# Attention weights scaled before they are transposed, a bit search counted by two engines in turn, and a sink as a column of the logits

## What is computed

```
def sink_softmax(logits, sinks):
    m = max(max(logits, axis=-1), s)
    e = exp(logits - m)
    return e / (sum(e, axis=-1) + exp(s - m))
# A: _, sel = top_k(scores, topk);  p = softmax(q @ k_sel / 8 + bias);  o = p @ v_sel
# B: logits = q @ k / 8 + bias (window mask);  p = sink_softmax(logits, sinks);  o = p @ v
```

## Time and profile before

| | |
|---|---|
| median of 3 runs | 2345.16 us (2342.01 to 2346.71) |
| profiled execution | 2343.02 us, span of its profile 2341.2 us |
| prompt's attention of A, first maximum to first sample logits L836 | 596.6 to 731.8 us |
| prompt's attention of B, first logits to L912 | 1763.8 to 1844.5 us |
| TensorE busy over the span | 96% |

### The profile page before, as it was taken

How to read it: one execution, slowest core, us unless ns; L and a number is a source line. 1 busy time by engine, 2 the same in 40 slices (tenths; PEclk the granted TensorE clock), 3 DMA queues, 4 the chain that set the end, 5 groups by cost and what they waited for, 6 DMA issues and landing times.

```text
span 2341.2 us, 39794 instructions
## 1 busy us (share of the span) xinstructions
PE 2258.6 (96%) x14801; PEld 2029.8 (87%) x14819; DVE 1137.1 (49%) x1811; ACT 415.4 (18%) x848; POOL 1029.7 (44%) x622
## 2 busy tenths in 40 slices
PE   7999999999888899999999999999999999999997
PEld 6999989959666588999999999999996689999997
DVE  4544522488584546555512555542264465555311
ACT  3101000131554412010000101000015420101002
POOL 4546455414001024555555555555541055555552
PEclk9999999999799999999999999999999899999998
DMA  5435363535003433333223333322350023333221
GB/s 125 99 73 115 78 155 89 114 64 147 10 1 100 130 89 77 86 81 81 78 84 90 82 86 85 81 78 82 94 154 23 1 73 81 81 86 83 79 83 60
DMA packets 378042, 196.33 MB, mean 84 GB/s; under 512 B 66531, under 2 KB 374476, under 8 KB 377932
## 3 DMA queue, kind: packets, MB, share of 16 engines
q1 hardware_dynamic: 366108, 180.79, 31.3%
q10 hardware_dynamic: 11552, 13.71, 2.0%
q0 software_dynamic: 288, 0.56, 0.1%
HBM read 192.23 MB, written 11.64 MB: 87 GB/s over the span
## 4 chain that ended last, share of the span: by engine, by line
PE 61%; DVE 2%; ACTq 0%; ACT 0%; issue 0%; DVEq 0%
PE psum L594 17%; PE psum L597 11%; PE psum L595 10%; PE psum L593 10%; PE psum L596 9%; PE psum L749 1%; PE psum L775 1%; DVE XS L1448 1%; PE psum L745 1%; PE psum L789 1%; ACTq L1200 0%; PE psum L758 0%; DVE squares L1481 0%; PE psum L939 0%; PE psum L938 0%
## 5 line engine op out<-in xcount | busy, mean ns | idle before, releaser
L545 POOL CAST WSP<-WST 128x1024 fp32r<-128x1024 f32 (+1 forms) x305 | 310.5, 1018 | 1250.0 <-PE psum L597 1008.8
L547 POOL TENSOR_TENSOR WSP<-WST,WSP 128x1024 fp32r<-128x1024 f32 (+1 forms) x305 | 709.3, 2326 | 24.5
L594 PE MATMUL psum<-XS,WSP 128*128 128x512 f32 x1672 | 658.4, 394 | 0.0
L593 PE MATMUL psum<-XS,WSP 128*128 128x320 f32 x1672 | 520.4, 311 | 9.5 <-DVE XS L1448 4.3
L597 PE MATMUL psum<-XS,WSP 128*128 128x320 f32 x1672 | 522.7, 313 | 0.0
L595 PE MATMUL psum<-XS,WSP 128*128 128x320 f32 x1672 | 519.2, 311 | 0.0
L596 PE MATMUL psum<-XS,WSP 128*128 128x256 f32 x1672 | 474.0, 283 | 0.0
L596 PEld LDWEIGHTS psum<-XS,WSP 128*128 128x128 f32 x1672 | 314.8, 188 | 71.5
L593 PEld LDWEIGHTS psum<-XS,WSP 128*128 128x128 f32 x1672 | 321.4, 192 | 11.6 <-DVE XS L1448 5.2
L597 PEld LDWEIGHTS psum<-XS,WSP 128*128 128x128 f32 x1672 | 321.5, 192 | 0.0
L594 PEld LDWEIGHTS psum<-XS,WSP 128*128 128x128 f32 x1672 | 314.4, 188 | 0.4
(11 more groups left out here) (325 smaller groups left out, 2595.0 us busy)
## 6 DMA issues: line engine op xcount, KB each, us to landing
WST<-in_ffn_w_gate SPq DMA_DIRECT2D x168, 256.0 KB, 3.9
WST<-in_ffn_w_up SPq DMA_DIRECT2D x168, 256.0 KB, 3.9
WST<-in_ffn_w_down SPq DMA_DIRECT2D x192, 224.0 KB, 3.5
WST<-in_a_w_in SPq DMA_DIRECT2D x28, 256.0 KB, 4.4
kv0A<-in_cache_kv SPq DMA_DIRECT2D x48, 128.0 KB, 2.3
kv2A<-in_cache_kv SPq DMA_DIRECT2D x48, 128.0 KB, 2.3
WST<-in_b_w_in SPq DMA_DIRECT2D x20, 256.0 KB, 4.0
kscr<-in_cache_idx SPq DMA_DIRECT2D x128, 32.0 KB, 2.1
```

The source lines that it names most:

```text
L545: nc.gpsimd.tensor_copy(WSP[s][:, 0, 0:width], WST[s][:, 0:width]).then_inc(w_hi, 1)
L547: nc.gpsimd.tensor_tensor(WSP[s][:, 1, 0:width], WST[s][:, 0:width], WSP[s][:, 0, 0:width].bitcast(F32), ALU.subtract).then_inc(w_split, 1)
L593: mm(front, high, x[:, 0, 0:FRONT], start=first, stop=False)
L594: mm(split, high, x[:, :, FRONT:TOK], start=first, stop=False)
```

## The change

Three things are changed, in the prompt's attention and the search.

1. The weights are divided ahead of transposition. After the exponentials of u VectorE takes the two reciprocals of this unit and multiplies the two blocks of weights in place (`factors`, behind the maximum of u+1). TensorE transposes only then; its order in step u becomes logits(u+2), values(u-1), transposed(u). `row_scales`, `otok` and the products are gone, and the high and low parts are made from banks 6 and 7 directly, both high parts on ScalarE in A and in B.
2. In the search the counts of units 0 to 23 alternate: even units on ScalarE (12 counts), odd units on VectorE (12 counts).
3. In B the sink is a column of the bias strip (with one masked column beside it to keep the width even), so logits, maximum and exponentials have 258 or 130 columns, and the separate steps for the sink go.

Besides, `block_diagonal` of A moves to GpSimd, ahead of the attention; GpSimd's split of the output weights of A waits for the last scaled weights instead of the last logits; and the sample's logits of the new keys of A come behind three groups of key transposes.

```diff
+                def factors(u):
+                    r, i, g = units[u]
+                    dve.wait_ge(ms["p_set"], 2 * (u + 1))
+                    nc.vector.reciprocal(m["ri"][:, i, :, g], m["rs"][:, i, :, g]).then_inc(ms["ri_set"], 1)
+                    dve.wait_ge(ms["ri_set"], u + 1)
+                    for n in range(KVH):
+                        p = m["p"][:, u % 2, n, 0:key_range(L, i)[1]]
+                        ts(p, p, m["ri"][:, i, n, g:g + 1], None, ALU.mult).then_inc(ms["pn_set"], 1)
+
+                def low_part(r, h):
                     i = ORDER[L][r]
...
+                    dve.wait_ge(ms["oh_set"], 2 * r + h + 1)
+                    tt(XL[s], bank[6 + h].rearrange("p (g t) -> p g t", g=4), XH[s].bitcast(F32), ALU.subtract)\
+                        .then_inc(ms["ot_evac"], 1)
                 for u, (r, i, g) in enumerate(units):
...
-                    if g in (1, 2) and r:
-                        products(r - 1, (g - 1,))
...
+                    nc.vector.tensor_reduce(m["nm"][:, i, :, g], PS[u % 2][:, :, 0:nk], AX, ALU.max, negate=True)\
+                        .then_inc(ms["nm_set"], 1)
+                    if u:
+                        factors(u - 1)
+                    if g == 7:
+                        low_part(r, 0)
                     if g == 3 and r:
-                        parts(r - 1)
+                        low_part(r - 1, 1)
                     after(u)
```

```diff
 # TensorE
-                for u, (r, i, g) in enumerate(units):
-                    more = u + 2 < len(units)
-                    transposed(u)
-                    if g == GRP - 1:
-                        row_scales(r, i)
-                    elif more:
+                for u in range(len(units)):
+                    if u + 2 < len(units):
                         logits(u + 2)
                     if u:
                         values(u - 1)
-                    if g == GRP - 1 and more:
-                        logits(u + 2)
+                    transposed(u)
...
 # ScalarE
-                if FOUND + 1 + u <= SIGN_COUNTS:
+                if u in SIGN_UNITS:
                     count(FOUND + 1 + u)
...
+                    if g == 5:
+                        high_part(r, 0)
+                    if g == 1 and r:
+                        high_part(r - 1, 1)
...
 # the sample's attention of A on TensorE
-                new_logits()
                 keys(0, 0)
                 keys(0, 1)
                 keys(0, 2)
+                new_logits()
...
-BITS, SIGN_COUNTS, FOUND = 32, 16, 7
+BITS, FOUND, SIGN_UNITS = 32, 7, range(0, 24, 2)
+SIGNED = (*range(1, FOUND + 1), *(FOUND + 1 + u for u in SIGN_UNITS))
```

More of the change, by code:

```diff
@@ L557, in ffn, with block_diagonal @@
                         split(n0 + GU_CHUNKS + q, i, RING, DB * P)
+            def block_diagonal(m, ms):
+                pool.wait_ge(acc_evac, at["inA"][1] + A_CHUNKS + RING)
+                nc.gpsimd.memset(m["qbd"][:, :, :], 0.0).then_inc(ms["qbd_clear"], 1)
+                pool.wait_ge(ms["qbd_clear"], 1)
+                for n in range(KVH):
+                    h = slice(n * HD, (n + 1) * HD)
+                    dst = m["qbd"][h].rearrange("p b (n g t) -> p n g b t", n=KVH, g=GRP)[:, n]
+                    nc.gpsimd.tensor_copy(dst, m["qT"][h, :, SEQ:TOK].rearrange("p g (b t) -> p g b t", b=NB))\
+                        .then_inc(ms["qbd_set"], 1)
+                pool.wait_ge(ms["qbd_set"], KVH)
             ffn("ffn0")
@@ L569, in _ @@
                 .then_inc(MS["A"]["selb_in"], 16)
-            pool.wait_ge(MS["A"]["qk_ps"], NQT * GRP)
+            m, ms = mixers["A"], MS["A"]
+            block_diagonal(m, ms)
+            pool.wait_ge(MS["A"]["pn_set"], 2 * NQT * GRP)
             for t in range(ND):
@@ L1217, in exps, with high_part @@
                             .then_inc(ms["p_set"], 1)
[L1219 to L1227, removed]
+                def high_part(r, h):
                     i = ORDER[L][r]
[L1229 to L1232, removed]
+                    act.wait_ge(ms["pv_ps"], GRP * r + 4 * h + 4)
+                    fn(XH[:, 4 * h:4 * h + 4, i * P:(i + 1) * P], bank[6 + h].rearrange("p (g t) -> p g t", g=4), ACT.Copy)\
+                        .then_inc(ms["oh_set"], 1)
                 exps(0)
@@ L1558, in prompt_attention @@
                 units = [(r, i, g) for r, i in enumerate(ORDER[L]) for g in range(GRP)]
-                def row_scales(r):
-                    i = ORDER[L][r]
-                    dve.wait_ge(ms["p_set"], 2 * GRP * (r + 1))
-                    rs, ri = m["rs"][:, i], m["ri"][:, i]
-                    if L == "B":
-                        dve.wait_ge(ms["es_set"], r + 1)
-                        steps.done(tt(rs, rs, m["es"][:, :, :], ALU.add))
-                    nc.vector.reciprocal(ri, rs).then_inc(ms["ri_set"], 1)
@@ L2002 @@
 KV_SLOTS = 3
+SINK = {"A": 0, "B": 2}
+STRIP = {L: 2 * P + SINK[L] for L in "AB"}
 ORDER = {"A": (0, 1, 2, 3), "B": (3, 2, 1, 0)}
[L2004 removed]
+BITS, FOUND, SIGN_UNITS = 32, 7, range(0, 24, 2)
+SIGNED = (*range(1, FOUND + 1), *(FOUND + 1 + u for u in SIGN_UNITS))
 HALF_B = NB // 2
```

102 lines of the change are left out of this document (26 added, 76 removed).

## The result

The changed kernel takes 2364.88 us (median of 7 runs, 2354.09 to 2368.38) against 2345.16 us (7 runs, 2338.24 to 2348.10): the ratio is 1.0082, with a 95% interval of 1.0061 to 1.0103, 0.8% slower. Forecast were 2346.5 us, no change that can be measured, and a range from 2336 to 2357: the result lies 19.7 us above the kernel before and outside the range. The profiled execution took 2361.88 us with a span of 2360.1, 18.9 more than before's 2341.2.

What follows compares the result with a forecast made beforehand. TensorE was taken to bound B, and a serial circle of search, scaling and TensorE steps to bound A's rounds 0 to 2. B -10.8, A +8.6, clock +3.3 made +1.1 us on 2345.16: 2346.5, range 2336 to 2357.

Steps and rivals of the forecast that it cites:

- I take two of the eight gaps: 3.3: A, rounds 1 and 2: TensorE's clock falls after two of eight waits, each costing up to 1.7 us; 3.3 us in all.
- the clock falls at every gap: Rival, A: all eight gaps pay 1.7 us instead of two, 10.2 us more, total 2356.5 us; chance 0.20.
- -10.8 + 8.6 = -2.2 us: Terms before the clock's: B's attention 10.8 us shorter, A 8.6 us longer.
- A's circle: A, rounds 0 to 2: search and attention steps wait in series; a unit pair takes 8.1 us, 9.2 in round 2.
- The scaling's price: VectorE, each unit: reciprocal with wait 0.20 us, multiplications 0.20, 0.27, 0.35, 0.42 for 128, 256, 384, 512 elements.
- F: VectorE's scaling of one unit's weights: 0.55, 0.70, 0.86, 1.0 us for 128, 256, 384, 512 keys.
- The rival of a dear scaling: Rival: multiplications cost one element per cycle and VectorE holds TensorE at B's low parts; 2351 us, chance 0.15.
- where 10.8 stood: B: spread sums and round-end extras go, scaling hides beside TensorE; ends at 1834 instead of 1844.5, gaining 10.8 us.
- the 698.4 of A: A: forecast start of round 3's first maximum, 2.0 us before 700, against 685.4 before: 13.0 us later.
- The other two signs of a wrong prediction: A pair shorter than 7.5 us in A, or a multiplication over 0.35 us with 256 elements.
- what was to show it right: B: 2.28 us steps, L912 10.8 earlier; A: pairs 8.1 and 9.2, `decide` waiting 2 or more, L836 9 to 12 later.
- shorter pairs: Rival, A: full clock in round 0, or scaling releases transposes without gaps lowering the clock; 2334 or 2339 us, chance 0.27.

Runs made afterwards that it cites:

- the gaps filled: Changed kernel plus twelve idle identity transposes on TensorE ahead of each odd unit's own transposes in rounds 0 to 2 of A: 2340.09 us, ratio 0.9993.
- one moved line: Changed kernel with ScalarE's count of unit u moved ahead of the exponentials of u+1 and the copy of u: 2313.22 us, ratio 0.9881 to the kernel before.
- the last experiment: Changed kernel with ScalarE's counts ahead of the exponentials, plus B's `qbd` filled by GpSimd instead of VectorE: ratio 0.9897 to the kernel before, one run left out.

## Why the prediction was wrong, step by step

**The step that failed is the clock: "I take two of the eight gaps: 3.3".** The eight pairs of rounds 1 and 2 are longer than with the gaps filled (from every second maximum) by 0.9, 2.4, 2.4, 0.0, 1.1, 1.3, 0.0 and 1.4 us in the profiled execution: 9.5, from 633.05 to 714.42 81.4 us for 71.9. Six of eight paid. In the second profile of the changed kernel all eight did, by 1.5 to 2.8: 15.4. And one gap costs 2.4 in round 1 where 1.7 was the most: nearly the whole piece of 3 us in the circle can run at half clock, not only its first part. Another 2.5 went in round 0, where filling raised the clock as well (from 0.54 to 0.72); the forecast had that round at the low clock, so this is no part of its error. Together it is 12.1 of A's 22.2 us in the one profile and 18.4 of 28.5 in the other (163.7 less 145.3), and 18 to 21 by the medians.

The profiles are 18.9 and 18.0 us above the one before, where 1.1 was forecast. Of that miss the clock in rounds 1 and 2 is 6.2 in the first (9.5 for 3.3) and 12.1 in the second, the largest term in both. The rest of A is 4.1 in the first, B 2.9, the way behind B, which the forecast left out, 3.4, and the scatter of the stretches ahead of A and between A and B 1.2.

The rival "the clock falls at every gap", 13.6 us, was the true mechanism, and its size lies between the 9.5 and the 15.4; its total of 2356.5 was still 8 us short. The Trainium skill, page "TensorE: Matmul & The Clock Gate", section on HAM oscillation, has the rule behind it, that a loop with a long wait in each turn starts each burst cold. By that rule, the trace agrees in part: in the first profile five of eight turns start at the low clock, one falls to it later and two don't. The first reason that I held against the rival was that waits of 1.5 to 1.8 us had not lowered the clock; the new waits are longer, 2.60 to 3.14. The second was that a gap shrinks when the work before it slows. It does, from 1.53 + 1.73 = 3.3 us to 2.6, and that was not enough.

**What the forecast says without the clock was near, and too low in both stages.** It was -10.8 + 8.6 = -2.2 us. With the gaps filled the kernel measured 0.07% under the one before, -1.6 us, but that agreement is in part luck: that kernel's A is 10.1 longer with a faster round 0, its B is 7.9 shorter and the way behind it 3.5 longer, which makes +5.6, and in its profile the stretch between A and B happens to be 5.5 shorter, within the scatter.

- *A's circle* was put at 8.1 a pair in rounds 0 and 1 and 9.2 in round 2. In the changed kernel the pairs of round 0 are 8.4, 8.1 and 8.1 (maxima at 599.59, 608.00, 616.10, 624.19), and the one across the round's end is 8.9; with the clock up those of round 1 are 8.1 to 8.7 and those of round 2 9.3 to 9.9. The first maximum of round 3 comes 114.8 after the first of round 0, 105.3 without the clock's 9.5; 102 was forecast. From there to the sample's logits it is 42.5 for 42.0. A without the clock in rounds 1 and 2: +12.7 measured, +8.6 forecast.
- *The scaling's price* was right where it matters: from the reciprocal at 642.73 to the next `decide` at 643.47 it is 0.74 with 256 keys, where F was 0.70. A single multiplication takes 0.28, 0.35, 0.42 and 0.48 us with 128, 256, 384 and 512 elements, 0.5 ns for each further element, where the maximum takes 1.04. The rival of a dear scaling is out.
- *B* gained 7.9 where 10.8 stood. By the forecast's own steps the end is at 1834.3, which is 10.2; the 10.8 was added up wrong by 0.6, and the 698.4 of A by 0.4 (700 less 2.0). The steps of 2.28 are there across round ends, as forecast. VectorE is late twice, though. First behind the fill of `qbd` (rows below), then at each low part: a maximum comes 2.95 after the one before and the next after 1.76, 0.15 more than two steps. 22 units take 51.3 for 50.2 (maxima at 1791.89 and 1843.18). The rest lies at the two ends and was not taken apart further; the last three products wait 0.53, 0.66 and 0.53 for copies on ScalarE.

VectorE in B of the changed kernel, in its timeline:

```profile
1793.47 0.91 DVE L1532 MEMSET qbdB<- 128x1024 f32 x1 [0.16 <-issue]
1794.42 0.86 DVE L1537 COPY qbdB<-qTB 64x512 f32<-64x512 f32 x2
1795.30 0.70 DVE L1566 TENSOR_REDUCE nmB<-psum 128x2 f32<-128x516 f32 x1
...
1805.45 0.69 DVE L1558 TENSOR_TENSOR XS<-psum,XS 128x512 fp32r<-128x512 f32 x1 [0.93 <-ACT XS L1218]
1806.06 0.69 DVE L1566 TENSOR_REDUCE nmB<-psum 128x2 f32<-128x516 f32 x1
```

The maximum at 1795.30 follows the fill without an idle time, 3.4 us after the one before it (1791.89). At B's end TensorE's clock is already down, and the sample's first transposes take nearly twice the 1.09 of the earlier trace rows:

```profile
1856.28 0.44 PE L789 MATMUL psum<-ptB,kvtokB 128*64 128x128 f32 x4 [0.53 <-ACT ptB L1235]
...
1859.42 0.69 PE L789 MATMUL psum<-ptB,kvtokB 128*64 128x128 f32 x4 [0.53 <-ACT ptB L1235]
1860.05 1.97 PE L907 MATMUL psum<-ident,kvB 128*128 128x128 f32 x8
```

Their window showed 0.57 above. That the waits of B's last units bring the clock down there was not tested with a run of its own, and it is not always so: the same B is followed by a clock of 0.57 in some profiles and of 0.64 to 0.75 in others.

**The signs that were named.** The clock under 0.75 in rounds 1 and 2 would make the prediction wrong; it was 0.78 and 0.88 in the profiled execution and 0.71 and 0.81 in the second profile. So in the first profile this sign didn't appear, and the forecast failed all the same. A limit on a round's mean was a poor sign: what counts is the clock in the part of each turn that stands in the circle, and there the length of the transposes, 1.12 or 0.66, tells it. The other two signs of a wrong prediction didn't appear either: no pair was shorter than 7.5, and a multiplication of 256 elements takes 0.35, just on the line. Of what was to show it right, `decide` did wait more than 2 us for ScalarE's count (4.50), but L836 came 22.2 us later within its stage instead of 9 to 12, and L912 7.9 us earlier instead of 10.8.

**The rival "shorter pairs"** is out for the changed kernel (round 0 took what was forecast), but its mechanism was the way to gain: not a faster TensorE but TensorE out of the circle. The forecast's own sum said so, with ScalarE's copy and the transposes between the count on VectorE and the one on ScalarE, and I did not ask what it would be worth to take them out.

## What to carry to other kernels

A serial chain of small steps that is hidden in the programs of several engines runs through everything that stands ahead of its steps in their queues. Write out the circle, with each engine's queue in it, and put a step of the chain ahead of the bulk work whose inputs come late: here one moved line was worth 2.0%, more than either part of the change. And once TensorE is in such a circle, price its work at the lower clock for every turn with a wait in it as long as those here (2.0 to 3.1 us), unless a row of that loop shows the clock to hold. Here six of eight turns paid in one execution and all eight in another, so a range fits such a term better than a number.

## What the runs showed of the hardware

In rounds 1 and 2 TensorE's clock held at 1.00 through waits of 1.42 to 1.73 us a turn with idle transposes ahead of them. Without these the waits were 2.60 to 3.14 us, and the clock fell in six of eight turns and held in two (3.06 and 2.94). The transposes of an identity that nothing reads were enough to keep it there; in round 0 the same filling gave 0.72.

Some VectorE instructions are held up while a GpSimd instruction runs. The step of `decide` on one number per partition takes 0.16 us, and once 3.99, in the kernel before (at 587.25) as in the changed one (VectorE, then GpSimd in the timeline):

```profile
589.88 3.99 DVE L1801 SCALAR_TENSOR_TENSOR seekA<-seekA 128x1 int32<-128x1 int32 x1
```

```profile
589.16 4.69 POOL L576 TENSOR_TENSOR WSP<-stripA,stripHA 128x2048 fp32r<-128x2048 f32 x1 [1.66 <-PE psum L609]
```

It ends at 593.87, as GpSimd's does at 593.85. The in-place multiplications of the last experiment are the second case, 3.46 for 0.61 the pair. The Trainium skill, page "SBUF — State Buffer", section "Who interferes with whom", names both kinds, those with two SBUF inputs and `tensor_scalar` in a two-port mode; both traces agree. So the scaling brought a new kind of instruction that GpSimd can hold up. Nothing came of it in the changed kernel, where GpSimd was idle in nearly all of A's and B's attention (8.06 and 1.97 us busy): no multiplication there took more than 0.49 us.
